# RWKV-7 chunked recurrence: zero-padded head pairs against even and odd heads on the two row halves of the matmul array

## What the reference computes

```python
def _wkv_step(s, inp):
    r, w, k, v, a, b = inp
    sa = jnp.einsum('bhvk,bhk->bhv', s, a)
    s = s * w[:, :, None, :] + sa[..., None] * b[:, :, None, :] + v[..., None] * k[:, :, None, :]
    return s, jnp.einsum('bhvk,bhk->bhv', s, r)
```

## Time and profile before

| | |
|---|---|
| median of 3 runs | 1007.4 us (1003.8 to 1007.82) |
| the profiled execution | 1004.92 us, span from first to last instruction 1003.1 us |
| mean granted TensorE clock | 0.932 |
| TensorE busy | 867.9 us (87% of the span) |
| weight loads / VectorE / ScalarE / GpSimd busy | 556.6 / 351.4 / 169.9 / 130.8 us |

### The profile page before, as it was taken

One profiled execution on the slowest core, in us unless ns is written; L12 is line 12 of the kernel. 1 busy time (PEld: TensorE's weight loads), 2 busy tenths in 40 slices (PEclk: granted clock), 3 DMA queues, 4 the chain that ended last, 5 costly groups with the idle time before them and its releaser, 6 DMA issues. The chain is left out here.

```text
span 1003.1 us, 10637 instructions
## 1 busy us (share of the span) xinstructions
PE 867.9 (87%) x4335; PEld 556.6 (55%) x4335; DVE 351.4 (35%) x595; ACT 169.9 (17%) x292; POOL 130.8 (13%) x196
## 2 busy tenths in 40 slices
PE   2998999899999998999999978698878787861996
PEld 2886888688888877467764433333323233321442
DVE  3226765797004423518231145311101010104443
ACT  3214320000022220032001013011010101011233
POOL 0001374401101030300000000201010101010000
PEclk9999999999979999799999979699989899895998
DMA  9121222213410020031810059389999999975001
GB/s 268 46 65 42 64 81 66 61 51 116 116 43 1 2 43 23 26 84 43 298 55 10 0 188 422 126 336 422 420 420 419 421 419 420 400 292 204 10 22 68
DMA packets 69594, 165.85 MB, mean 165 GB/s; under 512 B 7722, under 2 KB 47862, under 8 KB 57125
## 3 DMA queue, kind: packets, MB, share of 16 engines
q1 hardware_dynamic: 63581, 151.44, 40.1%
q0 software_dynamic: 5968, 13.77, 4.5%
HBM read 155.34 MB, written 17.90 MB: 173 GB/s over the span
## 5 line engine op out<-in xcount | busy, mean ns | idle before, releaser
L916 PE MATMUL PB<-hT,ring 128*128 128x272 f32 x1088 | 258.4, 400 | 0.0
L916 PEld LDWEIGHTS PB<-hT,ring 128*128 128x128 f32 x1088 | 210.4, 194 | 44.8 <-DVE pooled L816 0.3
L1790 PE MATMUL PB<-wexp,BIG 128*64 128x512 f32 x512 | 132.0, 675 | 38.0 <-DMA wexp<-in_expert_up 25.3
L1790 PEld LDWEIGHTS PB<-wexp,BIG 128*64 128x64 f32 x512 | 45.4, 155 | 113.7 <-issue 113.4
L1631 DVE TENSOR_TENSOR BIG<-BIG,PB 128x256 f32<-128x256 f32 x16 | 6.8, 422 | 211.3 <-ACT BIG L1452 211.3
L916 PE MATMUL PB<-pooled,ring 128*128 128x272 f32 x256 | 60.2, 393 | 0.9 <-DVE pooled L825 0.9
L1812 PE MATMUL PQ<-wexp,BIG 128*64 128x512 f32 x256 | 58.4, 598 | 1.2 <-ACT BIG L1456 1.2
L1145 PE MATMUL PQ<-ARBK,merged 128*128 128x512 f32 x128 | 55.2, 593 | 1.6 <-DVE merged L832 1.6
L1861 PE MATMUL PQ<-wexp,mhT 128*128 128x512 f32 x128 | 56.5, 601 | 0.0
L916 PEld LDWEIGHTS PB<-pooled,ring 128*128 128x128 f32 x256 | 48.6, 190 | 11.2 <-DVE pooled L825 1.3
L1145 PEld LDWEIGHTS PQ<-ARBK,merged 128*128 128x128 f32 x128 | 24.3, 190 | 32.2 <-issue 30.1
(11 more groups left out here) (368 smaller groups left out, 1035.8 us busy)
## 6 DMA issues: line engine op xcount, KB each, us to landing
wexp<-in_expert_gate SPq DMA_DIRECT2D x16, 2048.0 KB, 15.5
wexp<-in_expert_up SPq DMA_DIRECT2D x16, 2048.0 KB, 24.3
wexp<-in_expert_down SPq DMA_DIRECT2D x16, 2048.0 KB, 25.4
ring<-in_w_in SPq DMA_DIRECT2D x34, 512.0 KB, 4.1
BIG<-in_x_prompt SPq DMA_DIRECT2D x8, 512.0 KB, 11.5
ARBK<-in_w_out SPq DMA_DIRECT2D x1, 4096.0 KB, 13.6
hd<-BIG SPq DMA_DIRECT2D x8, 512.0 KB, 5.4
wexp<-in_w_ple_gate SPq DMA_DIRECT2D x1, 4096.0 KB, 13.2
```

What stands on the lines that cost most here:

```text
L916: last = pe.matmul(PB[n % 2][:, h, 0:HT], w, x[:, h * HT:(h + 1) * HT], start=(k == 0), stop=(k == len(ops) - 1))
L1790: last = pe.matmul(bank[2][64 * e:64 * e + 64, :].rearrange("p (q f) -> p q f", q=2), xgT[x][:, k, 64 * e:64 * e + 64], gu, start=(k == 0) ...
```

## The change

In the changed kernel no operand of these steps holds zeros for the other head. Each head has its own matmul that contracts over its own 64 partitions. Even heads use rows 0 to 63 of the array, odd heads rows 64 to 127, one after the other. Outputs of the two go to the two partition halves of one bank (lines 934, 1007, 1016, 1031) or, where they have the same partitions, to two banks (lines 977 and 1025). The off-diagonal block does the same with 32-row strips. `az`, `ARZ`, their copies and clears, and `split_heads` are gone. The first pass has one mask operation on 128 partitions into `GM`; the stores and loads around the inverse are split by even and odd heads, four for two and six for three. The state `S0` is [128, block, 64], and is added and scaled in one operation each. The right-hand side is copied as [128, 256]; the solution, now in two banks, is copied out in two operations. TensorE waits for its own `from_values` (`values_product_ready`) before it adds the state's part to the same bank. `gram_ready` rises by two at the end of the Gram products instead of by one at each half.

```diff
-    az = [view(0, 512 * k, 512).rearrange("p (j q t) -> p j q t", j=J, q=2) for k in range(2)]
-    MDs = view(1, 0, C * H * 32, 64).rearrange("p (n t) -> p n t", t=32)
-    MOs = view(3, 0, C * H * 32, 32).rearrange("p (n t) -> p n t", t=32)
+    GM = view(3, 0, C * J * 64).rearrange("p (n t) -> p n t", t=64)
...
-    RHS = view(7, 0, 512, 64)
-    S0z = view(7, 512, 512).rearrange("p (j q v) -> p j q v", j=J, q=2)
+    RHS = view(7, 0, 256)
+    S0 = view(7, 512, 256).rearrange("p (j v) -> p j v", j=J)
...
-        pool.memset(az[0], 0.0)
-        pool.memset(XTi, 0.0)
-        link(pool.memset(az[1], 0.0))
-        for c in range(C):
-            if c >= 2:
-                pool.wait_ge(pass1_products, c - 1)
-            link(pool.tensor_copy(az[c % 2][0:64, :, 0, :], ARp[0:64, :, c, 0, :]))
-            pool.tensor_copy(az[c % 2][64:128, :, 1, :], ARp[64:128, :, c, 0, :]).then_inc(a_split, 1)
-            pool.wait_ge(a_split, c + 1)
+        link(pool.memset(XTi, 0.0))
...
-        pool.dma_start(mmd[0:64].rearrange("q s t -> s q t"), MDs[0:32]).then_inc(triangles_stored, 16)
-        pool.dma_start(mmd[64:128].rearrange("q s t -> s q t"), MDs[32:64]).then_inc(triangles_stored, 16)
-        pool.wait_ge(triangles_stored, 32)
+        for q in range(2):
+            pool.dma_start(mmd[q:64:2].rearrange("n s t -> s n t"), GM[64 * q:64 * q + 32, :, 0:32]).then_inc(triangles_stored, 16)
+            pool.dma_start(mmd[64 + q:128:2].rearrange("n s t -> s n t"), GM[64 * q + 32:64 * q + 64, :, 32:64]).then_inc(triangles_stored, 16)
+        pool.wait_ge(triangles_stored, 64)
...
-        pool.dma_start(XT[0:32, :, 0:32], xtd[0:64].rearrange("q j t -> j q t")).then_inc(inverses_loaded, 16)
-        pool.dma_start(XT[32:64, :, 32:64], xtd[64:128].rearrange("q j t -> j q t")).then_inc(inverses_loaded, 16)
-        pool.dma_start(XA, xnd[0:64].rearrange("q s j -> s q j")).then_inc(inverses_loaded, 16)
-        pool.memset(XT[32:64, :, 0:32], 0.0).then_inc(inverse_buffer_set, 1)
+        for q in range(2):
+            pool.dma_start(XT[64 * q:64 * q + 32, :, 0:32], xtd[q:64:2].rearrange("n j t -> j n t")).then_inc(inverses_loaded, 16)
+            pool.dma_start(XT[64 * q + 32:64 * q + 64, :, 32:64], xtd[64 + q:128:2].rearrange("n j t -> j n t")).then_inc(inverses_loaded, 16)
+            pool.dma_start(XA[64 * q:64 * q + 32], xnd[q:64:2].rearrange("n s j -> s n j")).then_inc(inverses_loaded, 16)
+        link(pool.memset(XT[32:64, :, 0:32], 0.0))
+        pool.memset(XT[96:128, :, 0:32], 0.0).then_inc(inverse_buffer_set, 1)
...
-            nc.scalar.activation(SAV[c % 2][64:128], bank[1][64:128, :], ACT.Copy).then_inc(solution_taken, 1)
+            by_head = SAV[c % 2][64:128].rearrange("p (j q v) -> p q j v", j=J, q=2)
+            nc.scalar.activation(by_head[:, 0], bank[1][64:128, 0:256].rearrange("p (j v) -> p j v", j=J), ACT.Copy)
+            nc.scalar.activation(by_head[:, 1], bank[2][64:128, 256:512].rearrange("p (j v) -> p j v", j=J), ACT.Copy).then_inc(solution_taken, 1)
...
-            v.tensor_tensor(MDs[0:32, c * H:(c + 1) * H, :], g[0:32, :, 0:32], up[0:32].unsqueeze(1).to_broadcast([32, H, 32]), ALU.mult)
-            v.tensor_tensor(MDs[32:64, c * H:(c + 1) * H, :], g[32:64, :, 32:64], up[32:64].unsqueeze(1).to_broadcast([32, H, 32]), ALU.mult)
-            v.tensor_copy(MOs[0:32, c * H:(c + 1) * H, :], g[0:32, :, 32:64]).then_inc(pass1_masked, 1)
+            v.tensor_tensor(GM[:, c * J:(c + 1) * J, :], g, strict.unsqueeze(1).to_broadcast([P, J, 64]), ALU.mult).then_inc(pass1_masked, 1)
...
-            v.tensor_tensor(Stmp[0:64], st[0:64], S0z[0:64, :, 0, :], ALU.add)
-            link(v.tensor_tensor(Stmp[64:128], st[64:128], S0z[64:128, :, 1, :], ALU.add))
+            link(v.tensor_tensor(Stmp, st, S0, ALU.add))
...
-                v.tensor_tensor(S0z[0:64, :, 0, :], Stmp[0:64], gl[0:64], ALU.mult)
-                v.tensor_tensor(S0z[64:128, :, 1, :], Stmp[64:128], gl[64:128], ALU.mult).then_inc(state_ready, 1)
+                v.tensor_tensor(S0, Stmp, gl, ALU.mult).then_inc(state_ready, 1)
...
-            for j in range(J):
-                last = pe.matmul(bank[4 + c % 2][0:64, j * 128:(j + 1) * 128], BKp[:, j, c, 1, :], az[c % 2][:, j].rearrange("p q t -> p (q t)"), start=True, stop=True)
+            for h in range(H):
+                j, rows_q = h // 2, slice(64 * (h % 2), 64 * (h % 2) + 64)
+                last = pe.matmul(bank[4 + c % 2][rows_q, j * 64:j * 64 + 64], BKp[rows_q, j, c, 1, :], ARp[rows_q, j, c, 0, :], start=True, stop=True)
...
+        for r in range(2):
             for n in range(16):
-                i = 16 * r + n
-                last = pe.matmul(bank[4 + r % 2][32:64, n * 32:n * 32 + 32], MOs[0:32, i, :], XA[0:32, i, :], start=True, stop=True)
+                for q in range(2):
+                    rows_q = slice(64 * q, 64 * q + 32)
+                    last = pe.matmul(bank[4 + r][32 + 64 * q:64 + 64 * q, n * 32:n * 32 + 32], GM[rows_q, 16 * r + n, 32:64], XA[rows_q, 16 * r + n, :], start=True, stop=True)
...
-            for j in range(J):
-                last = pe.matmul(bank[4 + j // 2][:, (j % 2) * 256:(j % 2) * 256 + 256], BK[:, j, c * 128:(c + 1) * 128],
-                                 ARZ[c % 2][:, j].rearrange("p q x t -> p (q x t)"), start=True, stop=True)
-                if j % 2:
-                    last.then_inc(gram_ready, 1)
+            for h in range(H):
+                j, q = h // 2, h % 2
+                rows_q = slice(64 * q, 64 * q + 64)
+                last = pe.matmul(bank[4 + q][:, j * 128:j * 128 + 128], BK[rows_q, j, c * 128:(c + 1) * 128], AR[rows_q, j, c * 128:(c + 1) * 128], start=True, stop=True)
+            last.then_inc(gram_ready, 2)
...
-                pe.matmul(bank[0][0:64, h * 64:h * 64 + 64], Gs[k][0:64, h, 0:64], SAV[k][0:64, h * 64:h * 64 + 64],
-                          start=(h == 0), stop=False, skip_group_check=True)
+                j, q = h // 2, h % 2
+                last = pe.matmul(bank[0][64 * q:64 * q + 64, j * 64:j * 64 + 64], Gs[k][0:64, h, 0:64], SAV[k][0:64, h * 64:h * 64 + 64],
+                                 start=(h < 2), stop=False, skip_group_check=True)
+            last.then_inc(values_product_ready, 1)
...
             pe.wait_ge(state_ready, c + 1)
-            for j in range(J):
-                last = pe.matmul(bank[0][0:64, j * 128:(j + 1) * 128], ARp[:, j, c, 0, :], S0z[:, j].rearrange("p q v -> p (q v)"),
+            pe.wait_ge(values_product_ready, c + 1)
+            for h in range(H):
+                j, rows_q = h // 2, slice(64 * (h % 2), 64 * (h % 2) + 64)
+                last = pe.matmul(bank[0][rows_q, j * 64:j * 64 + 64], ARp[rows_q, j, c, 0, :], S0[rows_q, j, :],
                                  start=False, stop=True, skip_group_check=True)
...
-                last = pe.matmul(bank[1][64:128, h * 64:h * 64 + 64], XT[0:64, c * H + h, :], RHS[:, h * 64:h * 64 + 64], start=True, stop=True)
+                j, rows_q = h // 2, slice(64 * (h % 2), 64 * (h % 2) + 64)
+                out = bank[2][64:128, 256 + j * 64:320 + j * 64] if h % 2 else bank[1][64:128, j * 64:j * 64 + 64]
+                last = pe.matmul(out, XT[rows_q, c * J + j, :], RHS[rows_q, j * 64:j * 64 + 64], start=True, stop=True)
...
-            for j in range(J):
-                pe.matmul(bank[3][:, j * 64:j * 64 + 64], S0z[:, j].rearrange("p q v -> p (q v)"), ARp[:, j, c, 1, :],
+            for h in range(H):
+                j, rows_q = h // 2, slice(64 * (h % 2), 64 * (h % 2) + 64)
+                pe.matmul(bank[3][rows_q, j * 64:j * 64 + 64], S0[rows_q, j, :], ARp[rows_q, j, c, 1, :],
                           start=(j == 0), stop=False, skip_group_check=True)
```

More of the change, by code:

```diff
@@ L148, in mixer @@
     XNi = view(6, 1024, 1024).rearrange("p (s t) -> p s t", s=32)
[L149 to L153, removed]
+    XA = view(7, 0, C * J * 32).rearrange("p (n t) -> p n t", t=32)
+    XT = view(5, 0, C * J * 64).rearrange("p (n t) -> p n t", t=64)
+    P2T = view(1, 0, C * J * 32).rearrange("p (n t) -> p n t", t=32)
     Gs = [view(1, 1024 * k, 1024).rearrange("p (h x) -> p h x", h=H) for k in range(2)]
@@ L430, in _ @@
         pool.dma_start(xnd[0:64], XNi[0:64]).then_inc(inverses_stored, 16)
-        for c in range(2):
-            split_heads(c)
         pool.wait_ge(inverses_stored, 32)
-        pool.dma_start(XT[0:32, :, 0:32], xtd[0:64].rearrange("q j t -> j q t")).then_inc(inverses_loaded, 16)
-        pool.dma_start(XT[32:64, :, 32:64], xtd[64:128].rearrange("q j t -> j q t")).then_inc(inverses_loaded, 16)
-        pool.dma_start(XA, xnd[0:64].rearrange("q s j -> s q j")).then_inc(inverses_loaded, 16)
-        pool.memset(XT[32:64, :, 0:32], 0.0).then_inc(inverse_buffer_set, 1)
-        pool.wait_ge(inverse_buffer_set, 2)
[L439 to L443, removed]
+        for q in range(2):
[4 more added lines that the diff above has]
+        pool.memset(XT[96:128, :, 0:32], 0.0).then_inc(inverse_buffer_set, 1)
```

(48 more changed lines are left out.)

22 lines of the change are left out of this document (5 added, 17 removed).

## The result

The changed kernel took 980.99 us (median of 4 runs, 977.15 to 984.44) against 1007.61 for the kernel before on the same chip: a ratio of 0.9731, interval 0.9702 to 0.9759. A second set of runs gave 981.78 against 1008.22, 0.9735 [0.9708, 0.9763]. The forecast was 979, in a range of 969 to 994.

The account below looks back on a forecast made before the run. TensorE was taken to bound the projections and the recurrence. Gains of 4.5 + 4.0 + 16.9 + 1.7 = 27.1 us gave 977.8 from the profiled execution and 980.3 from the median, hence 979, range 969 to 994.

Parts of the forecast that it names:

- first pass: First pass over the chunks, without GpSimd's copies and with one mask operation: 4.5 us gained, bounds 2.5 and 6.
- block and first preparation: Off-diagonal block and first chunk's preparation, with quadrants alternating: 4.0 us gained, bounds 1.5 and 6.
- seven periods: Recurrence, seven full chunk periods: each falls from 8.45 to 6.03 us, 16.9 us gained in all.
- last chunk: Last, shorter chunk of the recurrence: 4.47 us against 6.15, 1.7 us gained.
- The pairing of row halves: Gram products (L977) alternating row halves run side by side: 1.01 us a chunk, 2.08 if weight loads queue.
- The rival without it: Row halves don't pair: L977 costs 2.08 us, period 7.66, gain 14 us, about 992 in all; chance 0.15.
- The period: One chunk of the recurrence on TensorE, from L1016 to the next L1016: 6.03 us, a gain of 2.42.
- the solution's part: From L1025 to L1037, with the solution copied by ScalarE in two operations: 1.56 us where it was 2.11.
- the state's chain: VectorE's two state operations between L1037 and L1016: 1.69 us from L1037's start, under TensorE's 1.83.
- The off-diagonal block: Its two groups of 128 small instructions, alternating quadrants: 32 ns each, 4.1 + 4.1 us, gaining 2.7.
- The loads: Stores and loads around the inverse: extra issues hidden under the projections, costing nothing; 6 us without that cover.
- the rival in which it falls for most of it: Clock at 0.50 for most of the recurrence: period 10.4 us, about 1015 in all; chance 0.06.

Follow-up runs that it names:

- first profile: Profiled execution of the changed kernel in its first set of runs: 982.39 us; median of that set 980.99 us, ratio 0.9731 to the kernel before.
- second profile: Changed kernel run again unaltered, for a second trace: profiled execution 986.53 us; median 981.78 us, ratio 0.9735 to the kernel before.
- the order of heads: Changed kernel with even heads first, then odd, in the first pass and five steps of each chunk: 999.02 us, 0.989 of the kernel before.
- Two kernels with the two runs apart: Changed kernel with the off-diagonal block's first half moved ahead of the last two projection groups: 977.52 us; the same plus Gram products moved earlier: 970.25 us.
- Gram products early: Changed kernel with Gram products moved one chunk ahead and `from_values` ahead of the wait for ScalarE: 976.02 us, 0.9682 of the kernel before.
- with 29 ns an instruction: Changed kernel with the off-diagonal block's even heads first, then the odd ones, instead of in turn: one run, 980.46 us.

## Why the prediction was right

The forecast's case came in, with the mechanism that it named, and its sum was close in the total and in most terms:

| term | forecast | first profile | second profile |
|---|---|---|---|
| first pass | 4.5 | 6.16 | 4.88 |
| block and first preparation | 4.0 | 4.04 | 3.53 |
| seven periods | 16.9 | 16.3 | 13.9 |
| last chunk | 1.7 | 1.8 | 1.8 |
| sum | 27.1 | 28.3 | 24.1 |

That the total came so near is in part luck: the first pass gave more than forecast in both profiles, the periods less, above all in the second, where the first of them ran largely at half clock.

**The pairing of row halves**, the step on which most hung and for which the trace of before had no row, held: 1.09 us for the Gram products (1.01 forecast), and the order of heads shows that it is the turn between tiles that does it. The rival without it was priced too high: instructions that stay on one tile take 54 and 102 ns, not 67 and 130, and the period is 7.42 where the rival had 7.66, though more groups stay on one tile. The time of that order, 999.02, is still above the rival's 992; its profiled execution took 993.19, with 3.7 us of that in a first period largely at half clock and 2.2 more in the block than the changed kernel has. What lengthens its other runs (up to 1002.52), no trace shows.

By the Trainium skill (TensorE: Matmul & The Clock Gate, Part 3, The mechanism), L980, which changes only the column half, would have stayed at 1.07. The trace after disagrees, as that of before did: its 16 instructions take 0.68 us from the first start to the last result, where they took 1.14.

**The period** is 0.09 longer than its sum: the Gram products and L992 cost 0.12 more, L980 with its wait 0.09 more, the solution's part 0.09 less, since ScalarE's second copy starts 0.28 and not 0.38 after the first; the wait is 0.32, not 0.5. That the state's chain stays under TensorE's work held with 0.26 to spare (0.14 forecast).

**The first pass** is the term that was mis-sized: of the 5.5 us worked out, 1.0 was held back for a half clock behind the wait. In the first profile the clock stayed at 1.00 and the pass gained 6.16, just past the bound of 6; in the second it fell and it gained 4.88. The kernel is the same in both, so the term has two values, and the forecast lies below the lower one. Of seven profiles with this code two kept the clock (6.73 us in both) and five lost it (7.78 to 8.01). Of the 0.66 by which the first profile passes the 5.5, 0.26 is VectorE, whose masks started 2.76 us after the stage's start and not 3.02 as before; the rest is that TensorE went on 0.06 us behind the first mask (178.22), where the sum had it wait for two.

**The off-diagonal block** was right in its sum and wrong in its parts: 8.09 us for the 256 small instructions, 8.2 forecast, but not as 256 times 32 ns. They take 17 ns, and the pause of 2.65 gives back what that gained; that the two cancel is luck. The half clock, for which 0.5 was held back, cost 0.47 in the first transposes (0.91 us for 0.44). Two kernels with the two runs apart show neither the pause nor the half clock, and the first of them gets 4.3 us. In six profiles of this order the pause ended 6.2 to 7.3 us after L932 began, always behind instruction 105.

The trace has more on it. In each of the six a packet of the instruction queue (16 KB) was in flight when TensorE stopped. This is the queue's row in the first profile, from 282.9 to 284.1 us (packets, MB, share of the DMA engines):

```profile
q8 instruction: 1, 0.02, 6.0%
```

That packet ran from 282.92 to 284.08; TensorE stopped at 283.01 and went on at 285.66. In the profile with the shortest pause (1.65, Gram products early) the packet ran from 284.78 to 285.82, the stop came at 285.66 and the end at 287.31. In all six TensorE went on 1.4 to 1.6 us after the packet had landed. So it did with 29 ns an instruction: there the packet landed at 287.13 and the 107th weight load started at 288.50, but the slower work left only 0.22 us to wait. With the two runs apart a packet landed as the first run ended and none fell within the second, and neither run shows a pause, so a packet in flight does not stop TensorE by itself. The pause thus reads as TensorE waiting for its next instructions, which it used up sooner at 17 ns each. The rows bear this out, but no run moved the packet alone, and the trace does not say whose instructions it held. A load of weights runs in the same microseconds, at up to 348 GB/s; it ran with 29 ns an instruction too (up to 347), so by itself it does not make a pause of this length.

**The loads** for the inverse were issued until 249 and landed 3.2 us later, more than 25 us before L932, so their extra issues cost nothing. **The clock** held 1.00 in the recurrence, but for the first chunk in four of nine profiles; the rival in which it falls for most of it did not come.

## What to carry to other kernels

Where a matmul group works on 64 rows or 64 columns of the array, let neighbours in the list take different tiles, and look at the order of the loop before looking at the shapes: here, by the medians, 18 of the 27 us went with the order. When products get shorter, look next at what stands behind each result that the same engine waits for (here 0.85 us a chunk) and put work with no such wait into that gap. Two long runs of very small instructions are better parted by other work, if a pause without a releaser stands in one; look there whether a packet of the instruction queue lands shortly before the pause ends.

## What was not expected of the hardware

- 32-by-32 matmuls in turn over two tiles went at 17 ns an instruction, 29 ns on one tile at a time.
- The pause without a releaser: 1.65 to 2.65 us in six profiles with 256 of these instructions in a row at 17 ns each, 0.22 where each took 29 ns, none where the two 128 were apart; in all seven TensorE went on 1.4 to 1.6 us after a 16 KB packet of the instruction queue had landed.
- The clock fell to 0.50 in or right behind the run of 256 in every profile that had it in one piece, with the long pause or without it; with the two runs apart it stayed at 1.00. Whether it is the length of the run or something else that goes with it, no run separates.
